# Columns of a product visited four at a time, from halves, quarters or 64-byte steps of a row, in five stages

## The reference, cut to what matters

```
first:  h += gla_mixer(rmsnorm(h));  h += swiglu(rmsnorm(h))      # gated linear attention, 4 heads
        h += dsa_mixer(rmsnorm(h));  h += swiglu(rmsnorm(h))      # sparse attention, 8 heads
second: h += retention(rmsnorm(h));  h += swiglu(rmsnorm(h))      # chunked retention, 4 heads
        h += mla_mixer(rmsnorm(h));  h += swiglu(rmsnorm(h))      # low-rank queries and keys, 8 heads
        return rmsnorm(h)[:, 16:]
```

## Time and profile before

| | |
|---|---|
| time of the profiled execution | 1350.57 us |
| its span from first to last instruction | 1348.8 us |
| around the span | 1.8 us |
| median of the runs | 1350.65 us |
| TensorE matmul busy | 1341.2 us, 99%, 9873 matmuls |
| TensorE weight loads busy | 1280.4 us, 95% |
| VectorE busy | 1009.2 us, 75% |
| ScalarE busy | 708.3 us, 53% |
| GpSimd busy | 296.7 us, 22% |
| granted TensorE clock | 1.000 of 2.4 GHz |
| read from HBM | 226.80 MB, 169 GB/s over the span |

### The profile page before, as it was taken

How to read it: one execution, slowest core, us unless ns; L and a number is a source line. 1 busy time by engine, 2 the same in 40 slices (tenths; PEclk the granted TensorE clock), 3 DMA queues, 4 the chain that set the end, 5 groups by cost and what they waited for, 6 DMA issues and landing times.

```text
span 1348.8 us, 24729 instructions
## 1 busy us (share of the span) xinstructions
PE 1341.2 (99%) x9873; PEld 1280.4 (95%) x9873; DVE 1009.2 (75%) x1613; ACT 708.3 (53%) x1167; POOL 296.7 (22%) x313
## 2 busy tenths in 40 slices
PE   9999999999999999999999999999999999999998
PEld 8999999999999888899999999999999999988886
DVE  6788766656997988778877876766557885898843
ACT  7565544444756555544444664544445565655543
POOL 1136000023152000132366744000022533120000
PEclk9999999999999999999999999999999999999999
DMA  8334665665443655565443455555554653566552
GB/s 279 127 125 157 192 191 184 193 187 162 137 158 129 216 190 193 168 198 188 160 138 126 155 187 160 187 169 176 172 172 145 191 157 127 168 203 191 194 183 77
DMA packets 220457, 229.72 MB, mean 170 GB/s; under 512 B 13664, under 2 KB 207704, under 8 KB 220344
## 3 DMA queue, kind: packets, MB, share of 16 engines
q1 hardware_dynamic: 219232, 226.24, 52.6%
q10 hardware_dynamic: 1112, 1.90, 0.6%
HBM read 226.80 MB, written 1.33 MB: 169 GB/s over the span
## 4 chain that ended last, share of the span: by engine, by line
PE 99%; DMA 0%; issue 0%; SPq 0%; DVE 0%; ACT 0%; DVEq 0%
PE ps L602 28%; PE ps L600 21%; PE ps L598 20%; PE ps L595 14%; PE ps L1160 2%; PE ps L1159 2%; PE ps L1161 2%; PE ps L661 1%; PE ps L663 1%; PE ps L662 1%; PE ps L929 1%; PE ps L799 1%; PE ps L1004 1%; PE ps L787 0%; PE ps L1092 0%; PE ps L886 0%
## 5 line engine op out<-in xcount | busy, mean ns | idle before, releaser
L1201 ACT ACTIVATE uh<-raw 128x1024 fp32r<-128x1024 f32 (+4 forms) x452 | 446.7, 999 | 433.7 <-PE ps L602 372.1
L1797 DVE TENSOR_TENSOR ul<-raw,uh 128x1024 fp32r<-128x1024 f32 (+3 forms) x448 | 528.2, 1187 | 131.2 <-PE ps L602 82.3
L602 PE MATMUL ps<-xx,ul 128*128 128x272 f32 (+1 forms) x2136 | 603.1, 282 | 0.0
L598 PE MATMUL ps<-xx,uh 128*128 128x272 f32 (+1 forms) x1448 | 419.1, 289 | 0.0
L600 PE MATMUL ps<-xx,uh 128*128 128x272 f32 (+1 forms) x1448 | 414.9, 287 | 0.0
L602 PEld LDWEIGHTS ps<-xx,ul 128*128 128x128 f32 x2136 | 402.3, 188 | 0.0
L598 PEld LDWEIGHTS ps<-xx,uh 128*128 128x128 f32 x1448 | 272.4, 188 | 3.0 <-issue 1.7
L600 PEld LDWEIGHTS ps<-xx,uh 128*128 128x128 f32 x1448 | 272.6, 188 | 0.8
L602 PE MATMUL ps<-aa,ul 128*128 128x272 f32 (+1 forms) x920 | 261.0, 284 | 0.0
L595 PE MATMUL ps<-xx,uh 128*128 128x512 f32 x704 | 244.7, 393 | 0.0
L598 PE MATMUL ps<-aa,uh 128*128 128x272 f32 (+1 forms) x788 | 226.7, 288 | 0.0
(11 more groups left out here) (343 smaller groups left out, 1645.1 us busy)
## 6 DMA issues: line engine op xcount, KB each, us to landing
raw<-in_ffn_w SPq DMA_DIRECT2D x62, 1024.0 KB, 5.3
raw<-in_ffn_w_in SPq DMA_DIRECT2D x44, 1024.0 KB, 5.3
raw<-in_ret_w_in SPq DMA_DIRECT2D x24, 1024.0 KB, 5.1
raw<-in_ffn_w_out SPq DMA_DIRECT2D x16, 1024.0 KB, 5.8
raw<-in_gla_w_in SPq DMA_DIRECT2D x11, 1024.0 KB, 5.3
raw<-in_ret_w_o SPq DMA_DIRECT2D x8, 1024.0 KB, 5.1
raw<-in_dsa_w_in SPq DMA_DIRECT2D x7, 1024.0 KB, 5.2
raw<-in_ffn_w_out SPq DMA_DIRECT2D x8, 768.0 KB, 4.8
```

Of the source, the lines that this page charges most:

```text
L598: e.matmul(in_turns(ps[:, 0:n1 - n0]), hi[:, k, :], in_turns(x.hi[:, k0 + j, n0:n1]), start=first and j == 0, stop=False)
L602: i = e.matmul(in_turns(ps[:, 0:n1 - n0]), lo[:, k, :], in_turns(x.hi[:, k0 + j, n0:n1]), start=False, stop=last and j == len(ks) - 1)
L1201: i = e.activation(unit_hi(u)[:, :, cols], a, ACT.Copy)
L1797: i = e.tensor_tensor(unit_lo(u)[:, :, cols], a, unit_hi(u)[:, :, cols].bitcast(F32), ALU.subtract)
```

## The change

`in_turns` gets a second argument, `walk`. With it, the row is cut into `walk` equal parts, and the view takes four columns (16 bytes) from the first part, four from the second and so on to the last, then the next four from the first. `Split` carries the number, and `norm_x` sets it: 2 for stages 0 and 2, 4 for stages 1 and 6, 17 for stage 4. For 272 columns the parts of walk 2 are 544 bytes apart, those of walk 4 272 bytes, those of walk 17 64 bytes; for 256 columns walk 2 has 512 bytes and walk 4 has 256. Stages 3, 5 and 7, and all products that read other `Split` objects, have no number and keep runs of eight. So does the first unit of stage 0 (`PACKED`). The number of instructions, their order, waits and sizes stay.

```diff
-def in_turns(v):
+def in_turns(v, walk=None):
+    if walk is not None:
+        return v.rearrange("p (c n q) -> p n c q", c=walk, q=4)
     return v.rearrange("p (n c q) -> p c n q", c=2, q=PIECE)

 class Split:
-    def __init__(self, pair, s_hi, s_lo, base=0):
+    def __init__(self, pair, s_hi, s_lo, base=0, walk=None):
+        self.walk = walk
         self.pair, self.hi, self.lo = pair, pair[:, 0], pair[:, 1]
         self.s_hi, self.s_lo, self.base = s_hi, s_lo, base

         def norm_x(i):
-            return Split(norm_rows(i), s_xh[i], s_xl[i])
+            return Split(norm_rows(i), s_xh[i], s_xl[i], 0, {0: 2, 1: 4, 2: 2, 4: 17, 6: 4}.get(i))

                     else:
-                        e.matmul(in_turns(ps[:, 0:n1 - n0]), hi[:, k, :], in_turns(x.hi[:, k0 + j, n0:n1]),
+                        e.matmul(in_turns(ps[:, 0:n1 - n0], x.walk), hi[:, k, :], in_turns(x.hi[:, k0 + j, n0:n1], x.walk),
                                  start=first and j == 0, stop=False)
-                        e.matmul(in_turns(ps[:, 0:n1 - n0]), hi[:, k, :], in_turns(x.lo[:, k0 + j, n0:n1]), start=False,
-                                 stop=False)
-                    i = e.matmul(in_turns(ps[:, 0:n1 - n0]), lo[:, k, :],
-                                 in_turns(x.hi[:, k0 + j, n0:n1]), start=False, stop=last and j == len(ks) - 1)
+                        e.matmul(in_turns(ps[:, 0:n1 - n0], x.walk), hi[:, k, :], in_turns(x.lo[:, k0 + j, n0:n1], x.walk),
+                                 start=False, stop=False)
+                    i = e.matmul(in_turns(ps[:, 0:n1 - n0], x.walk), lo[:, k, :],
+                                 in_turns(x.hi[:, k0 + j, n0:n1], x.walk), start=False, stop=last and j == len(ks) - 1)
```

## The result

The changed kernel took 1360.96 us (median of two runs, 1360.61 and 1361.32) against 1350.65 before: 0.76% slower, ratio 1.0076 with an interval of 1.0059 to 1.0093. The forecast was 1347.6 us, the range ended at 1357. The page of the changed kernel has as many instructions as the one before; TensorE alone took longer. The lines of the code have moved down by three: L601, L603 and L605 are what L598, L600 and L602 were.

A forecast was written before the change was run, and what follows sets the result against it. The prediction took TensorE's matmuls to bound the kernel: 3288 matmuls x 0.9 ns = 3.0 us less, so 1350.6 - 3.0 = 1347.6 us. The range for 8 in 10 was 1339 to 1357 us.

The forecast's parts named there:

- What bounds the kernel: Whole kernel: TensorE's matmuls set the pace, covering 99% of the span; the other engines have slack.
- The count: Stages 0, 1, 2, 4 and 6: 2856 matmuls of 272 columns and 432 of 256 change, 3288 in all.
- The bound on the order: Changed stages: doubling the breaks gains at most 1.8 ns or loses at most 1.1 ns a matmul.
- The term for 272 columns at 64 bytes: Forecast gain of 0.9 ns a matmul, taken for all 3288 changed matmuls, 3.0 us less on TensorE.
- the first rival: Changed stages: a new order only shifts how matmuls fall against each other; 4.3 us either way, 1346 to 1355; chance 0.29.
- the second rival: L598, L600, L602: each added break costs 0.42 ns, 46.3 us more, 1397 us; stage 4 alone, 1367 us; chance 0.12.
- The streaming loss: Rival, changed stages: parts far apart remove the loss while columns stream; 22.5 us less, 1328 us, or half, 1339; chance 0.11.
- The rule: Trainium skill, against the change: non-contiguous PSUM views slow matmuls significantly; SBUF's 16-byte lines need at least two hits each.

The follow-up runs named there:

- the scan: Variant of the changed kernel in which each unit of weights takes the next of eight column orders, for input and output alike; 1423.05 us, one run.
- the kernel for the period: Variant of the changed kernel: stage 7 reads x in 256-column matmuls, its units taking eight orders in turn, mostly two parts at different distances; 1374.81 us, one run.

## Why the prediction was wrong

- **What bounds the kernel** was right. TensorE's matmuls set the end before and after; the ten microseconds are the sum of the steps, and no wait, transfer or other engine took part.
- **The count** of 2856 and 432 matmuls was right, and so was the way to read the cost from starts.
- **The bound on the order failed, and it is the step on which all hung.** "I bound the effect of doubling them at a gain of 1.8 ns a matmul and a loss of 1.1 ns" treats the number of breaks as the variable, since the rows held only two orders, in order and runs of eight at 64 bytes. The runs showed the variable to be where in SBUF the next run lies. Two things were dear: steps that are a multiple of 256 bytes (+19.2 ns in stage 6), and a row read from two parts in turns (+6.5 ns at 544 bytes in stages 0 and 2), both together in stage 2 with 256 columns (+11.9). Neither order in the rows has either, so neither could bound them. What was measured in place of -1.8 to +1.1 ns: from -1.1 (64 bytes) to +19.2 (256 bytes). The mean over the 3288 matmuls is 10.3 us / 3288 = 3.1 ns.
- **The term for 272 columns at 64 bytes**, a gain of 0.9 ns, was right for stage 4 (1.1 measured) and for stages 0, 1 and 2 as soon as they had that step. The saving of runs of eight over none, 1.8 ns from starts rounded to 10 ns, is 0.9 from the unrounded starts of the same seven patterns in the trace of before (124.8 against 123.9) and 0.4 in the scan (125.0 against 124.6). So the term came out right as half of a reading that was twice too large, and that was luck.
- **Phase**, the first rival, doesn't explain this result: the changed kernel's values came back within 0.2 ns in the kernel with the orders on the input alone. Its range ended at 1355. But it was not the 2 ns that it was taken for: in the kernel for the period the same view cost 124.4 and 132.2 ns.
- **A price of a break**, the second rival, had the right side and the wrong mechanism. It named the 64-byte steps of stage 4 as the suspect; they were the only ones that gained.
- **The streaming loss** did not go. Of the 10.6 ns over pure columns at 272 columns, 9.5 are left at 64 bytes. That some order takes nearly all of it away was not seen; 1344-byte steps with 256 columns came to 114.9 ns, 8.2 over the columns' 106.7. Its premise, that successive groups can fall on the same place of the memory, was close to what the runs found. But it expected parts far from each other to avoid that, and parts 256 or 512 bytes apart bring it about.
- **The rule.** The Trainium skill (Advanced Engine Details and Errata, section Memory Cachelines) says that broken views of PSUM slow matmuls significantly. No such loss was seen here with runs of four or eight: 1350.91 us with the orders on the output alone. Its other half, that SBUF has lines of 16 bytes, agrees with the 236.8 and 225.9 ns for runs that take half a line or straddle two. But both have two hits on each line, which is what the section asks for, and they still cost about twice as much; the measurement decides.

The prediction's last sentence had named this way to fail, a loss that depends on the address more than runs of eight at 64 bytes could show, but gave it no chance and no share of the range.

The plain lesson is about the range. The code gave the distances, 544, 272, 512, 64 and 256 bytes, and two of them are multiples of 256. With no row that held a step of this kind, the bound should have said that it held for short steps alone, and the range should have reached further up. At worst a run cost 19.2 ns / 64 = 0.30 ns more, not far from the 0.42 ns that the second rival put on a break.

## What to carry to other kernels

In a dense stream of matmuls like this one, the order in which the input is read has a price: it should go by whole 16-byte lines, aligned, with successive lines on different residues modulo 256 bytes, and not from two parts in turns. Steps of 64 bytes were best within a row; steps that are multiples of 256 bytes, which halves and quarters of a power of two give, cost 11 to 24 ns of some 117, and 6 in one stretch. Read it from starts, as neither the busy share nor the durations show it. Put several orders into one kernel, unit by unit: one trace then compares them all. Let each order come round several times and look at every round, since one order can have two levels.

## What the runs showed of the hardware

- Reading two parts whose runs of four alternate: 132.2 ns for 256 columns at 256, 512, 1280 and 2560 bytes. Against 64 and 128 bytes (122.6, 123.3) each of the 32 repeated residues costs about 0.3 ns; with four parts at 256 bytes, against runs of eight, 17.7 ns / 48 = 0.37 ns. In the first round of the same kernel the price was under 0.1 ns (124.4 against 123.4 and 122.1).
- A run of four that lies on one line costs some 1.8 ns (122.8 / 68); one that straddles two, 225.9 / 64 = 3.5 ns.
- Writing PSUM in these orders costs nothing: 1350.91 us with the five orders on the output alone, against 1350.77.
- Open: why two parts at 64 or 128 bytes are 6 ns dearer than runs of eight at 64; why one view had two levels, 124.4 and 132.2 ns; why the same residues cost 125.6 ns in one kernel and 121.3 in another; what the 9.5 ns are that remain over 272 columns in the best order; and why in order costs 0.4 (272 columns) to 1.5 ns (256) more than runs of eight. Nothing was run for these.
